# The first 27 microseconds of a decoder step: zeros on TensorE, two engines scaling out of PSUM, and parameters turned after the first projection

## What is computed

```python
xn = rmsnorm(h, g_attn)              # x * rsqrt(mean(x*x) + eps) * g
z = xn @ w_in                        # queries, keys, values, gates, S5 input
q, kc, vc, ks, vs, kw, vw, gl, u, ga, gb = jnp.split(z, pts, axis=-1)
...
dt = jnp.exp(log_dt)[:, None]        # S5: a diagonal complex state
mag = jnp.exp(dt * ar)
ab_re = mag * jnp.cos(dt * ai)
ab_im = mag * jnp.sin(dt * ai)
...
y, hr, hi = ssm_scan(u, h0_re, h0_im, a_re, a_im, log_dt, b_re, b_im, c_re, c_im, d_skip)
```

## Time and profile before

| | us |
|---|---|
| median of 3 runs | 1084.92 |
| lowest, highest | 1084.85, 1087.29 |
| the profiled execution | 1085.54 |
| its span | 1083.9 |
| TensorE busy in the span | 1047.2 |
| VectorE busy | 726.1 |
| ScalarE busy | 317.1 |
| GpSimd busy | 256.9 |

### The profile page before, as it was taken

How to read it: one execution, slowest core, us unless ns; L and a number is a source line. 1 busy time by engine, 2 the same in 40 slices (tenths; PEclk the granted TensorE clock), 3 DMA queues, 4 the chain that set the end, 5 groups by cost and what they waited for, 6 DMA issues and landing times.

```text
span 1083.9 us, 21006 instructions
## 1 busy us (share of the span) xinstructions
PE 1047.2 (97%) x8127; PEld 924.8 (85%) x8127; DVE 726.1 (67%) x1629; ACT 317.1 (29%) x997; POOL 256.9 (24%) x401
## 2 busy tenths in 40 slices
PE   7999999999999999999999999999999999999996
PEld 5888777778899999988888778777898999999985
DVE  5999706646788888795644866355387888786442
ACT  4445524521222211101335364344012112210021
POOL 4854411003151111341342535010022111110000
PEclk9999999999999999999999999999999999999998
DMA  9645673334486555443546448442355556545331
GB/s 244 210 118 137 186 257 92 83 118 141 135 201 178 159 156 160 160 128 112 185 123 189 121 132 269 145 97 78 118 155 153 159 158 172 177 137 182 115 116 41
DMA packets 218260, 162.54 MB, mean 150 GB/s; under 512 B 25408, under 2 KB 212254, under 8 KB 218080
## 3 DMA queue, kind: packets, MB, share of 16 engines
q1 hardware_dynamic: 208928, 145.72, 45.8%
q0 software_dynamic: 4480, 13.27, 4.3%
q10 hardware_dynamic: 4752, 2.20, 0.8%
HBM read 157.94 MB, written 7.58 MB: 153 GB/s over the span
## 4 chain that ended last, share of the span: by engine, by line
PE 81%; DVE 12%; issue 2%; ACT 2%; DMA 1%; SPq 1%; POOL 0%; DVEq 0%; POOLq 0%; ACTq 0%
PE bank_dve L845 33%; PE bank_act L845 29%; PE bank_dve L1384 9%; DVE kT L2107 2%; PE bank_dve L1161 1%; PE bank_act L1236 1%; PE bank_o L1251 1%; DVE pcw L2114 1%; DVE Sf L2096 1%; PE bank_o L1203 1%; DVE vpast L2110 1%; DVE vpast L2104 1%; ACT L1500 1%; DMA R<-in_x_prompt_dram 1%; DVE Sf L2111 1%
## 5 line engine op out<-in xcount | busy, mean ns | idle before, releaser
L845 PE MATMUL bank_act<-xn,ring 128*128 128x264 f32 x928 | 215.6, 391 | 3.0 <-DVE xn L2071 2.0
L845 PEld LDWEIGHTS bank_act<-xn,ring 128*128 128x128 f32 x928 | 174.8, 191 | 39.4 <-issue 9.1
L845 PE MATMUL bank_dve<-sg,vpast 128*128 128x132 f32 x1008 | 123.6, 278 | 0.0
L845 PEld LDWEIGHTS bank_dve<-sg,vpast 128*128 128x128 f32 x1008 | 117.0, 190 | 1.6 <-DVE R L2408 0.4
L845 PE MATMUL bank_dve<-xn,ring 128*128 128x132 f32 (+1 forms) x672 | 85.7, 281 | 0.0
L845 PEld LDWEIGHTS bank_dve<-xn,ring 128*128 128x128 f32 x672 | 81.3, 190 | 1.2
L845 PE MATMUL bank_dve<-sg,ring 128*128 128x132 f32 (+1 forms) x480 | 69.1, 291 | 0.4 <-DVE sg L2298 0.4
L845 PEld LDWEIGHTS bank_dve<-sg,ring 128*128 128x128 f32 x480 | 62.4, 190 | 2.5 <-DVE sg L2298 0.5
L845 PE MATMUL bank_act<-ring,xn 128*128 128x256 f32 (+1 forms) x256 | 60.5, 389 | 0.0
L845 PEld LDWEIGHTS bank_act<-ring,xn 128*128 128x128 f32 x256 | 47.4, 190 | 8.8 <-issue 0.4
L1500 ACT ACTIVATE PT<-z 128x10 f32<-128x10 f32 x40 | 9.0, 224 | 144.7 <-DVEq L2448 144.7
(11 more groups left out here) (474 smaller groups left out, 2115.7 us busy)
## 6 DMA issues: line engine op xcount, KB each, us to landing
ring<-in_w_up_dram SPq DMA_DIRECT2D x88, 512.0 KB, 5.1
ring<-in_w_in_dram SPq DMA_DIRECT2D x28, 1024.0 KB, 6.0
ring<-in_w_down_dram SPq DMA_DIRECT2D x16, 1024.0 KB, 5.1
ring<-in_w_glu_dram SPq DMA_DIRECT2D x16, 512.0 KB, 4.6
ring<-in_w_o_dram SPq DMA_DIRECT2D x8, 1024.0 KB, 5.1
ring<-in_w_ple_gate_dram SPq DMA_DIRECT2D x8, 1024.0 KB, 5.2
ring<-in_w_down_dram SPq DMA_DIRECT2D x8, 768.0 KB, 4.5
PT<-in_cache_cmp_dram SPq DMA_DIRECT2D x64, 64.0 KB, 2.6
```

The source lines that it names most:

```text
L845: ins = pe.matmul(out, lhsT, rhs, start=(k == 0), stop=(k == nk - 1))
```

## The change

TensorE gets six matmuls of zeros before and between the transposes of the beginning: 448 columns each, from `qpad`, which GpSimd has set to zero, into `bank_o`, which nobody reads then. ScalarE and VectorE each write their own tiles twice out of PSUM, once plainly into `hT` and once times the gain into `hgT`; VectorE's `gained` goes, and the bank is given back after the second write. `params_turned` moves from the end of the beginning to behind job 0. VectorE adds the squares first and copies the parameters and works out the angles afterwards. The parameters' bank is now counted as a stage of layer 0 (`DVE_PRO` 6 becomes 5).

```diff
-ACT_PRO, DVE_PRO = 4, 6
+ACT_PRO, DVE_PRO = 4, 5
...
-        ("norm0", 1), ("c", 2 * own), ("k0", own), ("h0", own),
+        ("params", own), ("norm0", 1), ("c", 2 * own), ("k0", own), ("h0", own),
...
-    return 6 if L == 0 else dve_jobs(L - 1, "down", 3 + 1)
+    return dve_jobs(0, "params", 1) if L == 0 else dve_jobs(L - 1, "down", 3 + 1)
...
             def prologue(L, act_bank, dve_bank, next_chunk, mm):
+                def zeros(n):
+                    for _ in range(n):
+                        pe.matmul(bankO[:, 0:448], qpad[:, 0:P], qpad[:, P:P + 448], start=True, stop=True)
+                pe.wait_ge(zeroed, 1)
+                zeros(2)
                 pe.wait_ge(ident_in, 32)
                 pe.wait_ge(g_in, 16)
                 pe.transpose(dve_bank()[:, 0:KD], prm_rows[0:KD, :], ident[0:KD, 0:KD]).then_inc(dve_ready, 1)
+                zeros(1)
                 pe.wait_ge(x_in, 32)
                 for k in range(KD):
                     if k == 2:
+                        zeros(1)
                         pe.wait_ge(x1_in, 16)
                     if k == KD // 2:
+                        zeros(2)
                         pe.wait_ge(x2_in, 16)
...
-                params_turned(0, dve_bank)
...
                     if jobs == SUM_AT[L]:
+                        if L == 0:
+                            params_turned(0, dve_bank)
                         sum_squares(0)
...
+            act_.wait_ge(dve_freed, 1)
             for k in range(0, KD, 2):
-                fn(hT[:, k, :], take(0)[:, 0:NT]).then_inc(act_freed, 1)
+                bank = take(0)
+                fn(hT[:, k, :], bank[:, 0:NT])
+                fn(hgT[k], bank[:, 0:NT], scale=prm2[:, 0, k:k + 1]).then_inc(act_freed, 1)
...
             for k in range(1, KD, 2):
-                x_tile(k)
+                bank = take(0)
+                dve.tensor_copy(hT[:, k, :], bank[:, 0:NT])
+                ts(hgT[k], bank[:, 0:NT], prm2[:, 0, k:k + 1], None, MUL).then_inc(dve_freed, 1)
                 dve.wait_ge(act_freed, (k + 1) // 2)
                 dve.wait_ge(dve_freed, n[0])
-                gained(0, 0, k - 1)
-                gained(0, 0, k)
+                dve.sem_inc(hg_ready, 2)
             prep_steps(0)
-            prep_params(0, 0)
-            for k in range(KD):
-                add_squares(0, 0, k)
-            prep_angles(0)
...
+                if L == 0:
+                    for k in range(KD):
+                        add_squares(0, 0, k)
+                    prep_params(0, base)
+                    prep_angles(0)
                 norm(0)
```

More of the change, by code:

```diff
@@ L2033, in _ @@
             dve.wait_ge(ident_in, 32)
-            def x_tile(k):
-                dve.tensor_copy(hT[:, k, :], take(0)[:, 0:NT]).then_inc(dve_freed, 1)
             dve.tensor_copy(prm2[:, 0, 0:KD], take(0)[:, 0:KD]).then_inc(dve_freed, 1)
+            dve.wait_ge(dve_freed, 1)
             for k in range(1, KD, 2):
-                x_tile(k)
+                bank = take(0)
+                dve.tensor_copy(hT[:, k, :], bank[:, 0:NT])
+                ts(hgT[k], bank[:, 0:NT], prm2[:, 0, k:k + 1], None, MUL).then_inc(dve_freed, 1)
                 dve.wait_ge(act_freed, (k + 1) // 2)
                 dve.wait_ge(dve_freed, n[0])
-                gained(0, 0, k - 1)
-                gained(0, 0, k)
+                dve.sem_inc(hg_ready, 2)
             prep_steps(0)
-            prep_params(0, 0)
-            for k in range(KD):
-                add_squares(0, 0, k)
-            prep_angles(0)
             dve.sem_inc(h_done, KD)
```

## The result

| us | before | changed |
|---|---|---|
| median of 11 runs each, side by side | 1085.35 | 1088.97 |
| lowest, highest | 1082.86, 1089.20 | 1086.59, 1092.10 |
| ratio, 95% interval | | 1.0028 [1.0015, 1.0040] |
| the profiled execution, its span | 1085.54, 1083.9 | 1088.57, 1086.9 |

A forecast was written before the change was run, and what follows sets the result against it. The beginning was taken as bound by TensorE's columns and by VectorE's work hanging on ScalarE's roots, up to 42.03. 0.8 of wait gone plus 0.7 of earlier roots gave 1.5: 1084.92 - 1.5 = 1083.4, range 1081.3 to 1086.5.

The forecast's parts named there:

- nothing behind it depends on the beginning other than through it: After VectorE's copy of the C matrix: its row sets the time until 91.21, so the 1.5 gained reaches the end.
- the rival of the low-clock stretches: Later in the program: a shift may remove or bring a low-clock stretch, 1.7 either way; 8% beyond the other cases.
- Job 0 at 12.7: TensorE's beginning: tiles transposed by 11.8 and scaled by 12.7, chunk 0 landed at 12.5, so job 0 can begin.
- Job 0 in 3.65, the clock up early: TensorE: zeros raise the clock to 2.4 GHz early, so job 0 takes 3.65 in place of 5.64.
- The zeros' prices, 0.8 to 1.6: TensorE's beginning: one zero matmul of 448 columns takes 1.6 at the low clock and 0.8 at the high one.
- Products out of PSUM, 0.43 and 0.48: Scaling of the tiles: one product out of PSUM takes 0.43 on VectorE and 0.48 on ScalarE.
- Exponential at 17.2: ScalarE, after the parameters turned behind job 0: exponential at 17.2, 1.9 later than before, against a slack of 1.95.
- the second rival: The rival called "nothing reaches the end", with the exponential at 18.0 instead of 17.2; 20%.
- Issue 1.6 for the second key load: ScalarE's queue between exponential and roots: issue takes 1.6 instead of 2.30, bounds 0.4 and 2.3, roots 0.7 earlier.
- Roots at 20.9, VectorE at 40.5: ScalarE's roots at 20.9 against 21.59; VectorE goes on at its copy of the C matrix at 40.5, not 42.03.
- nothing reaches the end: Rival: exponential at 18.0, issue keeps 2.30, roots 0.8 late, VectorE at 42.0; total 1084.9, 0.3 around it; 20%.
- 0.8 of VectorE's wait gone: Ahead of VectorE's copy of the C matrix: its 0.80 wait for TensorE disappears, 0.8 of the 1.5 gain.

The follow-up runs named there:

- e6: Kernel before plus six two-column zero matmuls (24 instructions) at the start of TensorE's program; 1088.16, ratio 1.0018 [1.0000, 1.0036].
- e13: Changed kernel plus two tiny memsets ahead of VectorE's program; 1089.62, one execution.
- e9: Changed kernel untouched, run once more; 1087.98, ratio 1.0013 [1.0000, 1.0026] against the kernel before.
- e1: Kernel before with zeros and scaling out of PSUM, parameters still turned ahead of job 0; 1087.53, ratio 1.0014 [0.9994, 1.0035].
- e2: Changed kernel without its six zero matmuls; 1088.35, ratio 1.0017 [1.0005, 1.0028] against the kernel before.
- e3: Changed kernel with two unused 448-column matmuls filling TensorE's idle time between job 2 and the columns; 1088.01, ratio 1.0025 [1.0013, 1.0038].
- e12: Kernel before with only the six zero matmuls added; 1085.33, ratio 0.9993 [0.9980, 1.0007].
- e5: Kernel before untouched, run again against itself; 1087.42, ratio 1.0001 [0.9986, 1.0017].
- e4: Changed kernel with ScalarE's layer 0 key loads issued behind its copies of job 2; 1087.88, ratio 1.0003 [0.9991, 1.0016].
- e14: Changed kernel plus eight tiny memsets ahead of VectorE's program; 1086.98, one execution.

## Why the prediction was wrong

- **The failed step: "nothing behind it depends on the beginning other than through it."** Two things do. TensorE's instruction fetches fall elsewhere, and one meets SyncE's issues: 0.72 and 0.77 in the two traces (e6 shows the cause). VectorE's instructions stand elsewhere, and three starts come late: 1.13 and 1.02 by TensorE's offset (e13 shows the cause). These 1.8 us have no line in the sum; the rival of the low-clock stretches saw only that a shift can move things, and not these. Up to 91.21 the step held: what VectorE had won or lost at its copy of the C matrix, TensorE has at 107 within 0.1 or 0.2 (1.22 and 1.36, -0.96 and -0.86).
- **Job 0 at 12.7: wrong by 1.0.** It started at 13.69, after the landing of `pt_sb` at 13.65. The prediction took the small tables as landed by 12.5, since no small packet ran between 12.5 and 13.0; a gap of half a microsecond was read as an end. In the same trace of before 15 packets under 512 bytes ran between 13.0 and 14.5. Behind the transposes and products, the last at 13.83, job 0 would not have come much sooner: in e9 it waited for ScalarE's last product and started at 13.64. This was also a term of the sum: the tiles ended at 12.8, not 11.8, as the last two zeros ended at 11.0 (9.25 + 1.77) and not 10.2 and a tile took about 0.5 (0.53 from 11.32 to 11.85) and not 0.40.
- **Job 0 in 3.65, the clock up early: right.** 3.72 in the chain. The zeros' prices, 0.8 to 1.6, held as well (3.36 for the first two, 1.02 for the fourth).
- **Products out of PSUM, 0.43 and 0.48: right for ScalarE, small for VectorE,** 0.48 on both; VectorE's product out of SBUF took 0.31.
- **Exponential at 17.2: it came at 18.07,** 0.9 late, and so at the turning point of the second rival. Job 0's start makes 1.0 of it.
- **Issue 1.6 for the second key load: mis-sized.** 2.47, above the bound of 2.3 that was taken from one row. From exponential to roots it is 4.39, as in before (4.35). In other traces both loads together took 1.03 (e1), 1.09 (e2), 1.66 (e3), 1.95 (e9), 3.13 (e12), 3.26 (e5); no packet of an instruction queue lay on any of them, so the fetch is not the cause, and what is stays open. The step's form was right, its range was too narrow, and e4 shows the remedy: take the issue off the way.
- **Roots at 20.9, VectorE at 40.5: 22.46 and 43.25 in the first trace, 21.44 and 41.07 in the second.** The rival "nothing reaches the end" has roots 0.8 late and the prediction falls by its own words at 22.4. The first trace adds the stretch at 26.6, 1.7, which the prediction had only as a stretch "later on". Over the five traces with the changed kernel's beginning the means are: exponential at 18.1 instead of 17.2, second load's issue 2.0 instead of 1.6, roots at 22.0 instead of 20.9. These two terms, 1.3 together, are most of the forecast gain of 1.5, gone before anything behind the beginning is lost; the outcome up to there is the rival "nothing reaches the end".
- **0.8 of VectorE's wait gone: right.** In the changed kernel no wait stands ahead of its copy of the C matrix.

In numbers, for the first profiled execution: against the predicted gain of 1.5 it lost 3.0, a difference of 4.5. Of this 2.9 is the beginning (1.36 instead of -1.5), 0.7 the fetch, 1.1 the late starts, and -0.2 the stretches between. In the second trace the beginning takes 0.6 of it (-0.86), so part of the 2.9 is the luck of one execution.

## What to carry to other kernels

An edit that adds or drops instructions on an engine moves everything behind it in that engine's program, and costs or gains can turn up at places that it does not touch; so follow the offset between two traces over the whole span before you judge the edit, and if it jumps where nothing was edited, try the same edit with a few idle instructions more or less. A DMA issue on the queue of an engine that is on the critical chain had no fixed price here, and belongs behind the work that others wait for. Compare at least two traces of each kernel before a microsecond of difference is given a cause.

## What was unexpected of the hardware

- The issue of a 64 KB load on SyncE's queue took 0.61 alone and 1.37, 1.44, 1.71, 1.79 and 1.84 where a 16 KB packet of TensorE's instructions was moved at the same time (changed, e9, e13, e4, e6). An issue that such a packet lengthened ended about 0.4 after the packet.
- 24 two-column matmul and weight-load instructions at the start cost 2.9 us a hundred microseconds later in one trace, 1.2 directly and 1.7 by the clock; by the medians the whole kernel lost 1.8 per thousand, with an interval from none to 3.6 (e6).
- VectorE began an operation 0.35 us late where it stood right behind a wait that had held it and was record 128n + 64 of VectorE's program: 38 times in 18 traces, and at no other number.
- The same two loads' issue on ScalarE's queue, ahead of the roots, took from 1.03 to 3.26 us, in one kernel (changed) 2.90 and 1.95.
- TensorE ran at 1.2 GHz for 3.4 us in the columns after an idle time of 2.16 (changed) and 2.00 (e14), and stayed at 2.4 after 1.92 (e13) and 1.13 (e9). Ahead of the parameter rows it was idle for 1.33 in e1 and fell to 1.2 GHz at 15.0, and for 1.67 in e12 and did not: the length of the idle time alone does not decide. Such stretches elsewhere come and go between executions of one kernel: two in before's first trace, three in its second, beside the one at the program's end.
